# The second layer's modulation moved into the first layer's retrieval, with another order in the output projections and mixers

## The reference, cut to what matters

```python
def _adaln(cvec, w, b):
    mod = jax.nn.silu(cvec) @ w + b
    return jnp.split(mod, 6, axis=-1)

def _gated_head_norm(o, gate, w):
    of = o.astype(f32)
    y = of * lax.rsqrt(jnp.mean(of * of, axis=-1, keepdims=True) + EPS)
    return y * w.astype(f32) * jax.nn.silu(gate.astype(f32))
...
for l in range(DEPTH):
    sh1s, sc1s, g1s, sh2s, sc2s, g2s = _adaln(c, ada_w[l], ada_b[l])
    hs = _modulate(_rms_norm(xs, norm1_w[l]), sh1s, sc1s)
...
    xs = xs + g1s[:, None, :] * ms
    hs = _modulate(_rms_norm(xs, norm2_w[l]), sh2s, sc2s)
    xs = xs + g2s[:, None, :] * _peer(hs, peer_w_q[l], peer_keys[l], peer_u[l], peer_v[l])
```

## Time and profile before

| what | us |
|---|---|
| median of 3 runs | 4584.6 |
| profiled execution | 4584.52 |
| its span | 4582.7 |
| TensorE busy | 4118.9 (90%) |
| VectorE busy | 3765.7 (82%) |
| GpSimd busy | 1991.2 (43%) |
| ScalarE busy | 1645.2 (36%) |
| setup | 0 to 160 |
| HGRN2 mixer, output projection | 160 to 722, to 843 |
| retrieval, routing, experts of layer 0 | to 1046, to 1210, to 2420 |
| GLA mixer, output projection | to 2876, to 2981 |
| retrieval, routing, experts of layer 1 | to 3184, to 3345, to 4555 |

### The profile page before, as it was taken

One profiled execution on the slowest core, in us unless ns is written; L12 is line 12 of the kernel. 1 busy time (PEld: TensorE's weight loads), 2 busy tenths in 40 slices (PEclk: granted clock), 3 DMA queues, 4 the chain that ended last, 5 costly groups with the idle time before them and its releaser, 6 DMA issues. The chain is left out here.

```text
span 4582.7 us, 73015 instructions
## 1 busy us (share of the span) xinstructions
PE 4118.9 (90%) x24791; PEld 3713.0 (81%) x24791; DVE 3765.7 (82%) x6718; ACT 1645.2 (36%) x2314; POOL 1991.2 (43%) x1435
## 2 busy tenths in 40 slices
PE   7799986977899999999996887886899999999997
PEld 3588886875799999999985877884779999999996
DVE  7688883599788888999996787378978888899997
ACT  7545442213333333333333433221433333333333
POOL 3234331214545445566653221220744545556663
PEclk9899997988999999999997988897999999999998
DMA  9411112214999999999982110220799999999995
GB/s 373 148 47 56 55 33 75 61 32 96 290 364 361 363 360 357 365 361 362 362 314 68 53 38 22 83 72 11 178 335 363 362 363 361 359 364 363 361 362 209
DMA packets 616028, 1049.50 MB, mean 229 GB/s; under 512 B 229699, under 2 KB 388870, under 8 KB 615430
## 3 DMA queue, kind: packets, MB, share of 16 engines
q1 hardware_dynamic: 467814, 508.86, 32.7%
q0 software_dynamic: 147456, 536.94, 31.5%
q10 hardware_dynamic: 672, 2.62, 0.1%
HBM read 982.75 MB, written 65.54 MB: 229 GB/s over the span
## 5 line engine op out<-in xcount | busy, mean ns | idle before, releaser
L1946 POOL DMA_INDIRECT rows_ex<-in_peer_v,ctx_index x512 | 708.2, 1383 | 476.2 <-DVE row_acc_ex L2021 360.6
L1946 POOL DMA_INDIRECT rows_ex<-in_peer_u,ctx_index x512 | 586.6, 1146 | 630.6 <-DVE dots_ex L2024 503.3
L2107 PE MATMUL pu_ex<-h_hi,uT_hi_ex 128*128 128x384 f32 x2048 | 715.9, 350 | 1.9 <-ACT coef_ex L1971 1.0
L2021 DVE SCALAR_TENSOR_TENSOR row_acc_ex<-rows_ex,factor_ex,row_acc_ex 128x1024 f32<-128x1024 f32 x512 | 657.6, 1284 | 52.7 <-issue 11.1
L2107 PE MATMUL pu_ex<-h_lo,uT_hi_ex 128*128 128x384 f32 x2048 | 693.0, 338 | 0.0
L2107 PE MATMUL pu_ex<-h_hi,uT_lo_ex 128*128 128x384 f32 x2048 | 693.0, 338 | 0.0
L2115 PE MATMUL py_ex<-v_hi_ex,c_hi_ex 128*128 128x512 f32 x1536 | 622.6, 405 | 0.0
L2024 DVE CUSTOM_DVE_ANT_0 rows_ex<-rows_ex,h_row_ex 128x1024 f32<-128x1024 f32 x512 | 604.5, 1218 | 0.0
L2115 PE MATMUL py_ex<-v_lo_ex,c_hi_ex 128*128 128x512 f32 x1536 | 601.3, 391 | 0.0
L2115 PE MATMUL py_ex<-v_hi_ex,c_lo_ex 128*128 128x512 f32 x1536 | 601.1, 391 | 0.0
L2012 DVE TENSOR_TENSOR uT_lo_ex<-pT_ex,uT_hi_ex 128x512 fp32r<-128x512 f32 x512 | 352.0, 687 | 178.1 <-ACT uT_hi_ex L1960 170.2
(11 more groups left out here) (435 smaller groups left out, 8508.5 us busy)
## 6 DMA issues: line engine op xcount, KB each, us to landing
u_raw_ex<-in_peer_u SPq DMA_DIRECT2D x256, 512.0 KB, 6.9
v_raw_ex<-in_peer_v SPq DMA_DIRECT2D x256, 512.0 KB, 6.2
ada<-in_ada_w SPq DMA_DIRECT2D x24, 2048.0 KB, 9.4
gates<-stage_ro SPq DMA_DIRECT2D x12, 4096.0 KB, 16.0
g_raw_ex<-gates SPq DMA_DIRECT2D x256, 192.0 KB, 6.2
w_raw_hgrn<-in_hgrn_w_in SPq DMA_DIRECT2D x40, 512.0 KB, 4.2
w_raw_re<-in_peer_w_q SPq DMA_DIRECT2D x32, 512.0 KB, 3.7
w_raw_gla<-in_gla_w_in SPq DMA_DIRECT2D x25, 512.0 KB, 4.0
```

Of the source, the lines that this page charges most:

```text
L1946: pool.indirect_dma_start(out=rows[m % RING][:, :], out_offset=None, in_=a["peer_u" if m < TG * NC else "peer_v"].rearrange("l n d -> (l n ...
L2021: nc.vector.scalar_tensor_tensor(row_acc[g][:, :], rows[j][:, :], factor[:, j:j + 1], row_acc[g][:, :], ALU.mult, ALU.add).then_inc(row_fr ...
L2107: last_ = nc.tensor.matmul(pu[:, 0:TD], w[:, k, :], x[:, k, 0:TD], start=(k == 0 and w is uT_hi[b] and x is h_hi), stop=(k == DC - 1 and w ...
```

## The change

- `setup` makes 12 blocks, layer 0's. `cs4` and `fold` become tensors of the whole kernel.
- `retrieve` in layer 0 makes layer 1's modulation in 16 pieces of 384 columns, one per half head. SP loads a piece (1.5 MB, two buffers); ScalarE makes its high part (`ada_high`), GpSimd its low part (`ada_low`), TensorE multiplies (`modulation`, 16 matmuls) and turns the row before (`turn_row`), ScalarE copies row and turned row. The high part, low part, product and row have one buffer each. VectorE adds the bias once at the end.
- `mix_out` in both layers makes all sums first, one inverse and one root, and then the spreads; the gates are loaded ahead of the weights; ScalarE's first two high parts come behind the root and GpSimd's first two low parts behind its fifth and sixth product; VectorE makes `low(k)` in step k instead of k+1.
- `mixer` in both layers has GpSimd's `lo(h, 2)` behind level 0 instead of behind level 2.

The diff, its two smallest hunks (the new tensors) and most unchanged lines left out:

```diff
--- before.py
+++ after.py
@@ -164,7 +165,7 @@
...
     NBL = 6 * D // NB
-    NALL = DEPTH * NBL
+    NALL = NBL
@@ -688,7 +688,9 @@
...
                     pool.drain().then_inc(pool_diff, 1)
-                for j in range(2, NCH):
+                    if l == 0 and (2 < L or not final):
+                        lo(h, 2)
+                for j in range(3, NCH):
@@ -1181,7 +1183,6 @@
...
     AHEAD = 2
-    GROUP = H // 2
@@ -1208,9 +1209,7 @@
...
-        rows = [pp[j][0][:, 0:GROUP * NT] for j in range(2)]
-        inv = [c["inv"][:, j * GROUP * NT:(j + 1) * GROUP * NT] for j in range(2)]
+        rows, inv = pp[0][0][:, 0:H * NT], c["inv"][:, 0:H * NT]
@@ -1221,12 +1220,10 @@
...
-            gates(0)
-            gates(1)
+            for i in range(4):
+                gates(i)
...
             weights(1)
-            gates(2)
-            gates(3)
@@ -1244,8 +1241,8 @@
...
                 pool.tensor_tensor(og[:, k, :], og[:, k, :], sg[:, k, :], ALU.mult).then_inc(gate_done, 1)
-                if k in (1, 2):
-                    low(k - 1)
+                if k in (4, 5):
+                    low(k - 4)
@@ -1262,17 +1259,12 @@
...
                     act.wait_ge(og_in[k // 2], 16)
-                if k == 4:
-                    high(0)
-                    high(1)
                 act.activation(sg[:, k, :], og[:, k, :], ACT.Sigmoid).then_inc(sig_done, 1)
-            for j in range(2):
-                act.wait_ge(inverted, j + 1)
-                act.activation(inv[j], inv[j], ACT.Sqrt).then_inc(rooted, 1)
-                if j == 0:
-                    act.wait_ge(y_done, 1)
-                    act.activation(h_hi[:, 0, :], y[0][:, :], ACT.Copy).then_inc(hi_done, 1)
-            for k in range(1, DC):
+            act.wait_ge(inverted, 1)
+            act.activation(inv, inv, ACT.Sqrt).then_inc(rooted, 1)
+            high(0)
+            high(1)
+            for k in range(DC):
@@ -1292,18 +1284,15 @@
...
                 for t in range(NT):
-                    col = g % GROUP * NT + t
                     for k in range(g * NV, (g + 1) * NV):
-                        last = nc.tensor.matmul(rows[g // GROUP][:, col:col + 1], sq[:, k, t * P:(t + 1) * P],
+                        last = nc.tensor.matmul(rows[:, g * NT + t:g * NT + t + 1], sq[:, k, t * P:(t + 1) * P],
...
             def spread(g):
-                pe.wait_ge(rooted, g // GROUP + 1)
...
                     dst = spread_s[g % 2][:, t, :] if t < NT - 1 else spread_c[g % 2][:, :]
-                    col = g % GROUP * NT + t
-                    last = nc.tensor.matmul(dst, inv[g // GROUP][:, col:col + 1].to_broadcast([P, P]),
+                    last = nc.tensor.matmul(dst, inv[:, g * NT + t:g * NT + t + 1].to_broadcast([P, P]),
@@ -1315,17 +1304,15 @@
...
-            for g in range(GROUP):
+            for g in range(H):
                 sums(g)
+            pe.wait_ge(rooted, 1)
...
             spread(1)
-            for g in range(GROUP, H):
-                sums(g)
...
                     if k == 0:
-                        pe.wait_ge(rooted, j + 1)
@@ -1348,13 +1335,6 @@
...
-            def inverse(j):
-                dve.wait_ge(summed, (j + 1) * GROUP)
-                nc.vector.tensor_scalar(inv[j], rows[j], float(D / mx.dv), EPS, ALU.mult, ALU.add)
-                dve.drain()
-                nc.vector.reciprocal(inv[j], inv[j])
-                dve.drain().then_inc(inverted, 1)
@@ -1371,21 +1351,19 @@
...
             dve.wait_ge(sq_dve, DC // 2)
-            gated(0)
-            gated(1)
-            inverse(0)
-            gated(2)
+            for k in range(3):
+                gated(k)
+            dve.wait_ge(summed, H)
+            nc.vector.tensor_scalar(inv, rows, float(D / mx.dv), EPS, ALU.mult, ALU.add)
             dve.drain()
+            nc.vector.reciprocal(inv, inv)
+            dve.drain().then_inc(inverted, 1)
...
                 normal(k)
-                if k == 0:
-                    inverse(1)
...
                     gated(k + 3)
-                if k >= 1:
-                    low(k - 1)
+                low(k)
                 dve.drain()
-            low(DC - 1)
@@ -1447,6 +1425,22 @@
...
         dve_passed = sem("dve_passed")
+        later = layer + 1 < DEPTH
+        AW = 6 * D // (2 * PH)
+        if later:
+            ada_w = a["ada_w"][layer + 1].rearrange("(k p) n -> p k n", p=P)
+            ada = [sb(f"ada{i}", [P, DC, AW]) for i in range(2)]
+            ada_hi = sb("ada_hi", [P, DC, AW], F32R)
+            ada_lo = sb("ada_lo", [P, DC, AW], F32R)
+            mod_row = sb("mod_row", [P, AW])
+            mod_raw = sb("mod_raw", [P, 48, 2])
+            pm = ps("pm", [P, 512])
+            ada_in = [sem(f"ada_in{i}") for i in range(2)]
+            ada_hi_done, ada_lo_done, ada_mm, row_out, row_turned, mod_done = (sem(n) for n in
+                ("ada_hi_done", "ada_lo_done", "ada_mm", "row_out", "row_turned", "mod_done"))
+        def turned_row():
+            return pm[:, AW:AW + 2 * AW // P].rearrange("p (i v) -> p i v", v=2)
@@ -1460,15 +1454,36 @@
...
                         .then_inc(k_loaded[b], 16)
+                    if later:
+                        sp.wait_ge(ada_lo_done, h * 2 + (b + 1))
+                        sp.dma_start(ada[b][:, :, :], ada_w[:, :, bass.ds(h * (2 * AW) + b * AW, AW)]) \
+                            .then_inc(ada_in[b], 16)
...
             pool.sem_inc(w_lo_done, 2)
-            with pool.Fori(0, PH) as h:
+            if later:
+                pool.sem_inc(ada_lo_done, 2)
...
+            def low(h, b):
+                pool.wait_ge(w_hi_done, h * 2 + (b + 1))
+                pool.tensor_tensor(w_lo[b][:, :, :], w_raw[b][:, :, :], w_hi[b][:, :, :].bitcast(F32),
+                                   ALU.subtract).then_inc(w_lo_done, 1)
...
+            def ada_low(h, b):
+                if later:
+                    pool.wait_ge(ada_hi_done, h * 2 + (b + 1))
+                    pool.tensor_tensor(ada_lo[:, :, :], ada[b][:, :, :], ada_hi[:, :, :].bitcast(F32),
+                                       ALU.subtract).then_inc(ada_lo_done, 1)
...
+            low(0, 0)
+            low(0, 1)
+            ada_low(0, 0)
+            with pool.Fori(0, PH - 1) as h:
                 for b in range(2):
-                    pool.wait_ge(w_hi_done, h * 2 + (b + 1))
-                    pool.tensor_tensor(w_lo[b][:, :, :], w_raw[b][:, :, :], w_hi[b][:, :, :].bitcast(F32),
-                                       ALU.subtract).then_inc(w_lo_done, 1)
+                    low(h + 1, b)
+                    ada_low(h + b, 1 - b)
+            ada_low(PH - 1, 1)
@@ -1489,18 +1504,57 @@
...
+            def ada_high(h, b):
+                if later:
+                    act.wait_ge(ada_in[b], h * 16 + 16)
+                    if not (isinstance(h, int) and h == 0 and b == 0):
+                        act.wait_ge(ada_mm, h * 2 + b)
+                    act.activation(ada_hi[:, :, :], ada[b][:, :, :], ACT.Copy).then_inc(ada_hi_done, 1)
...
+            def row(h, b):
+                if later:
+                    act.wait_ge(ada_mm, h * 2 + (b + 1))
+                    act.activation(mod_row[0:4, :], pm[0:4, 0:AW], ACT.Copy).then_inc(row_out, 1)
...
                     hi(0, 1)
-            with act.Fori(0, PH - 1) as h:
+            def turned_copy(h, b):
...
+                if later:
+                    act.wait_ge(row_turned, h * 2 + (b + 1))
+                    n = AW // P
+                    act.activation(mod_raw[:, bass.ds(h * (2 * n) + b * n, n), :], turned_row(), ACT.Copy).then_inc(mod_done, 1)
...
+            def halfway(h, b):
+                copies(h, b)
+                hi(h + 1, b)
+                if b == 1:
+                    turned_copy(h, 0)
+                elif not (isinstance(h, int) and h == 0):
+                    turned_copy(h - 1, 1)
+                row(h, b)
+                ada_high(h + b, 1 - b)
...
+            if later:
+                act.sem_inc(mod_done, 1)
+            ada_high(0, 0)
+            halfway(0, 0)
+            halfway(0, 1)
+            with act.Fori(1, PH - 1) as h:
                 for b in range(2):
-                    copies(h, b)
-                    hi(h + 1, b)
+                    halfway(h, b)
             copies(PH - 1, 0)
+            turned_copy(PH - 2, 1)
+            row(PH - 1, 0)
+            ada_high(PH - 1, 1)
             copies(PH - 1, 1)
+            turned_copy(PH - 1, 0)
+            row(PH - 1, 1)
+            turned_copy(PH - 1, 1)
@@ -1533,14 +1587,42 @@
...
             first_product(nc, pe, nm, pq, w_hi[0], w_lo[0], proj)
+            def modulation(h, b):
...
+                if later:
+                    pe.wait_ge(ada_lo_done, h * 2 + (2 + b + 1))
+                    if not (isinstance(h, int) and h == 0 and b == 0):
+                        pe.wait_ge(mod_done, h * 2 + b)
+                    for w, part in enumerate((ada_hi, ada_lo)):
```

(31 more changed lines are left out.)

## The result

| | us |
|---|---|
| before, median of 4 runs | 4582.8 |
| after, median of 4 runs (4612.43 to 4614.52) | 4613.95 |
| ratio | 1.0069, 95% interval 1.0057 to 1.0081 |
| span of the profiled execution after | 4612.7 (before 4582.7) |

What follows compares the result with a forecast made beforehand. Setup's engines run in step; VectorE's top-16 search paces layer 0's retrieval, then the piece chain. -64.7 + 70.5 - 21.5 - 6 + 20 + 4 = +2.3 us on 4584.5: 4587, range 4556 to 4616.

Steps and rivals of the forecast that it cites:

- rival B: Layer 0's retrieval: piece matmuls always at the lower clock, 5.1 instead of 3.0 us; +16 to +30, 4603 to 4617; chance 0.25.
- Setup: Setup: twelve of 24 blocks go, new end 94.75 us, -64.7; gain 60 if GpSimd's norm additions hold it.
- Output projection of layer 0: Layer 0's mix_out: terms start 8.6 us earlier and steps lose their h_lo wait; -21.5 (-15 to -25).
- Output projection of layer 1: Layer 1's mix_out: only the start is gained, later steps wait under 1 us; -6 (-3 to -8).
- Retrieval: Layer 0's retrieval: single buffers make the pieces a chain of 14.1 us each, which becomes the bound; +70.5 (+60 to +85).
- Rival C: Layer 0's retrieval: modulation hides in VectorE-bound slack, stage grows only 15 to 20, time near 4535; chance 0.06.
- The lower end of the retrieval: Layer 0's retrieval: with the chain fully overlapped, TensorE's 12.0 us per half head binds; put at +60.
- VectorE beside the 6.8 us subtractions: Layer 0's retrieval: GpSimd's 6.75 us subtractions could hold VectorE up to 108 us; counted at the tail only.
- HGRN2: HGRN2 mixer: per head 1.7 us of delayed factors plus 1.2 us for TensorE's lower clock, seven times; +20.
- the collision: HGRN2 mixer: a head's last GpSimd subtraction becomes due before VectorE's last factors, delaying them some 1.7 us per head.
- Rival A: Both mixers: the queue's move is free, 4587 - 24 = 4563; chance 0.22.
- GLA: GLA mixer: same move, four heads, levels beside VectorE's convolution; +1 per head, +4.

Runs made afterwards that it cites:

- the output projections alone: Kernel before with only the two changed output projections: 4556.1 us, ratio 0.9938.
- the chain cut: Changed kernel plus 32 bytes; TensorE signals after the high part's eight matmuls, so ScalarE makes the next high part earlier: 4580.2 us, ratio 0.9997.
- the queue's change alone: Kernel before with only GpSimd's first late weight subtraction moved behind level 0 in both mixers: 4610.9 us, ratio 1.0061.
- the same with the hold: Kernel before with the mixers' queue move, GpSimd also waiting in HGRN2 for line 987's factors before a head's last subtraction: 4586.2 us, ratio 1.0008.
- the pieces alone: Kernel before with only the modulation moved from setup into layer 0's retrieval, plus 32 bytes of pad: 4621.7 us, ratio 1.0083.

## Why the prediction was right or wrong

The forecast was 4587, a change too small to tell from none; measured were 4614, slower by 0.7%, inside the range of 4556 to 4616. That the range holds it is luck: it reached so far only for rival B, which did not happen, and the forecast's own span ended at 4604. Three of its four larger terms were right; a fifth, of 20 us, was missing.

- Setup, right: -64.7 against -64.66. GpSimd's additions didn't hold it.
- Output projection of layer 0, right in mechanism: -21.3 against -21.5, but the closeness is partly luck. The terms start 25.1 us behind the first sums (710.43 less 685.37) where 22.0 were worked out, for the eighty sums took 15.56 us instead of 14.6 and the first terms waited longer for `h_lo`. The eight steps then took 24.0 us instead of 26.8 (737.20 less 2.77 and 710.43). The two misses cancel.
- Output projection of layer 1: -8.8 against -6. With the output projections alone it was -5.2, with the queue's move in GLA alone and this stage unchanged -5.3, so not all of the 8.8 comes from the new order of its sums.
- Retrieval, right in mechanism and nearly in size: a chain, 14.07 us a piece against 14.1. Of the 4 us more, about 3 lie ahead of the end of the second piece (51.6 us behind the stage's start, 48.9 worked out) and about 2 in the fourteen periods behind it; three of these took 16.5, 15.5 and 15.5 us, each behind a piece whose low product ran at the lower clock (2.76, 2.76 and 2.61 us instead of 1.55). The old stage in turn ended at 1045.9, not 1044.7, which takes 1 off. That the chain of signals over the single buffers sets the pace is shown by cutting it: 11.99. Rival B, the matmuls at the lower clock every time, was wrong: the pauses of 1.8 to 1.9 us left 12 of the last 14 pieces at 1.55 us for eight matmuls. Its 4603 to 4617 holds the time by accident. Rival C needed overlap and was wrong as the chain stood.
- The lower end of the retrieval, +60, was worked out wrong: fourteen pieces at 12.0 instead of 14.1 us give 29 less, +41, and with the chain cut the stage grew by 37.8. Two smaller slips change nothing: eight steps of up to 3.3 us are 26.4 and not 26.8, and rival B's 15 x 1.1 to 2.1 is 16 to 32.
- VectorE beside the 6.8 us subtractions, which the prediction put at up to 108 us and counted at the tail only: its searches took as long as before, but its 24 additions of the candidates took 34 us in this stage instead of 7 (13 of them some 2.4 us each, where none had taken over 0.5). The chain hid these 27 us. With the chain cut they took 7 again.
- HGRN2, right in mechanism, too small: +27.7 against +20, and 25.6 to 27.7 in the five traces with this queue. TensorE's wait is 6.81 against "about 6", heads stand 66.6 to 68.2 apart against 66. The mis-sized term is the collision, put at 1.7 us per head: the factor was held 2.0, and undoing it took HGRN2 from +25.8 to +6.5, 2.8 per head. Where the other 0.8 come from is not shown. The 1.2 us for the clock were not too small: with the subtraction held back TensorE still waits 4.82 us and starts at the lower clock in every head, and all that stays is 0.9 per head. Rival A, a free move, fell.
- GLA, wrong in sign: +4 forecast; with its output projection it gives 7.3 with the queue's change alone. I costed the levels beside the convolution as a loss; which wait shrinks was not tested.
- The missing term, +20: I took `cs4` and `fold` for a change of names, and called routing and experts untouched. Their instructions are; their buffers' addresses are not. With +20 the forecast would have been 4607. The row that could have shown where to look is the write of 4 MB in 16.0 us in packets of 256 bytes, six in a stage and one every 18.1 us: it was 2 us away from setting the pace, and so sensitive to what its descriptors start at. The section of the Trainium skill, DMA: Bandwidth & Descriptors, that is named above gives the rule by which it could have been asked.

The sum of the stages is 30.0 us, the difference of the spans; no time is left over. The 5.9 to 7.4 us by which layer 0's unchanged output projection came out longer in three kernels (the queue alone, the same with the hold, the pieces alone), at a mean clock of 0.80 instead of 0.84, are not explained, and neither are the 2.9 us of the last experts.

## What to carry to other kernels

A tensor added to a pool from which all later buffers are allocated is a change of every stage: compare the start addresses of what small-packet DMAs read, and keep them at multiples of 256 bytes, as it paid here for packets of 256. Work moved into another stage's slack is a background only as far as its links overlap; count the chain per piece first, and signal a buffer free where its last reader ends, not where the whole product does. Of a 2.4 us subtraction on GpSimd, which can hold VectorE for its length, what counts is which VectorE instruction becomes due beside it: in both orders an operation of VectorE was held for some 2 us a head, yet HGRN2 differed by 19 us.

## What was not expected of the hardware

- 4 MB written in 256-byte packets from SBUF: 290 GB/s with the source at a multiple of 256 bytes, 218 at 32, 64, 128, 160 or 192 bytes behind one. A ratio of 1.33, the same at all five distances.
- The setup's loads, with packets of about 2 KB and in the other direction, into SBUF, don't show it: 383 GB/s between 34 and 80 us after and 386 before, while their buffers moved from 70400 (a multiple of 256) to 70560. Which of the two differences protects them was not tested.
- After waits of 1.8 to 1.9 us in every 14, TensorE's clock stayed at its upper level nearly throughout (0.99 in the window 850 to 970); after waits of 4.82 and 6.81 us it restarted at the lower one each time (ten 128-column products in 2.39 us instead of 1.31). After three waits of 2.1 us in the kernel before, the ten products took 2.35, 2.39 and 1.31 us.
